# Copying both heads' transposed probabilities with ScalarE, and reordering the columns of the second block

## What is computed

```
h  = rms_norm(x,  norm_g[i]) * (1 + sc)  + sh        # tokens
hc = rms_norm(xc, norm_g[i]) * (1 + scc) + shc       # context
u, z  = split(h  @ w_in)                             # q, k, v and the gate z
uc, zc = split(hc @ w_in)
# per head: p = softmax(q k^T * scale (+ bias in kind B));  o = p v
# kind C: a = p0 - lambda * p1, o = a v, then rms_norm(o)
x  = x  + gt  * ((o  * silu(z))  @ w_out)
xc = xc + gtc * ((oc * silu(zc)) @ w_out)            # not in the last layer
```

## Time and profile before

| | |
|---|---|
| median of 3 runs | 2235.68 us (2224.66 to 2236.77) |
| the profiled execution's own time | 2232.29 us |
| its span in the trace | 2230.5 us |
| mean granted TensorE clock | 0.951 of full speed |
| busy: PE, DVE, ACT, POOL | 2036.7, 1187.7, 1084.9, 933.0 us |
| instructions: PE, DVE, ACT, POOL | 14528, 2582, 2073, 598 |

### The profile page before, as it was taken

One profiled execution on the slowest core, in us unless ns is written; L12 is line 12 of the kernel. 1 busy time (PEld: TensorE's weight loads), 2 busy tenths in 40 slices (PEclk: granted clock), 3 DMA queues, 4 the chain that ended last, 5 costly groups with the idle time before them and its releaser, 6 DMA issues.

```text
span 2230.5 us, 39126 instructions
## 1 busy us (share of the span) xinstructions
PE 2036.7 (91%) x14528; PEld 1717.4 (77%) x14528; DVE 1187.7 (53%) x2582; ACT 1084.9 (49%) x2073; POOL 933.0 (42%) x598
## 2 busy tenths in 40 slices
PE   6899899988998999888999999998999899798787
PEld 5898799987987899776766886665788667567666
DVE  6854556658545566347673206667223766614553
ACT  5353566453634654454554336445334555535443
POOL 1574378004744682043452123443204455424443
PEclk9899999998999999999999999999999999899898
DMA  7353656653435566442123332222223211223211
GB/s 262 114 152 112 190 172 196 184 186 113 149 101 187 171 188 188 164 142 76 48 61 101 114 104 84 88 67 85 95 86 95 95 38 48 76 95 104 67 58 57
DMA packets 72991, 262.89 MB, mean 118 GB/s; under 512 B 8048, under 2 KB 10224, under 8 KB 72560
## 3 DMA queue, kind: packets, MB, share of 16 engines
q1 hardware_dynamic: 71536, 256.31, 36.6%
q0 software_dynamic: 1280, 4.20, 0.6%
HBM read 259.43 MB, written 1.05 MB: 117 GB/s over the span
## 4 chain that ended last, share of the span: by engine, by line
PE 68%; DVE 9%; issue 8%; POOL 7%; ACT 6%; DMA 1%; DVEq 0%; SPq 0%; ACTq 0%; POOLq 0%
PE gemm L458 15%; PE gemm L459 14%; PE gemm L460 14%; PE gemm L740 7%; POOL w_lo L298 3%; PE tbank L696 2%; PE score L781 2%; PE obank L839 2%; PE stat L703 1%; POOL rot L1970 1%; PE gemm L666 1%; PE stat L536 1%; ACT w_hi L1018 1%; PE stat L754 1%; PE score L786 1%
## 5 line engine op out<-in xcount | busy, mean ns | idle before, releaser
L298 POOL TENSOR_TENSOR w_lo<-ring,w_hi 128x1024 fp32r<-128x1024 f32 x262 | 628.6, 2401 | 721.8 <-ACT w_hi L1018 718.4
L458 PE MATMUL gemm<-g_hi,w_hi 128*128 128x256 f32 x1344 | 394.7, 294 | 29.2 <-DVE w_lo L298 10.8
L1018 ACT ACTIVATE w_hi<-ring 128x1024 fp32r<-128x1024 f32 x344 | 361.3, 1053 | 82.9 <-PE gemm L460 37.4
L458 PE MATMUL gemm<-h_hi,w_hi 128*128 128x512 f32 (+1 forms) x928 | 390.8, 421 | 4.7 <-POOL w_lo L298 4.7
L459 PE MATMUL gemm<-g_lo,w_hi 128*128 128x256 f32 x1344 | 384.0, 286 | 0.0
L460 PE MATMUL gemm<-g_hi,w_lo 128*128 128x256 f32 x1344 | 383.6, 285 | 0.0
L459 PE MATMUL gemm<-h_lo,w_hi 128*128 128x512 f32 (+1 forms) x928 | 352.6, 380 | 0.0
L460 PE MATMUL gemm<-h_hi,w_lo 128*128 128x512 f32 (+1 forms) x928 | 352.1, 379 | 0.0
L458 PEld LDWEIGHTS gemm<-g_hi,w_hi 128*128 128x128 f32 x1344 | 262.9, 196 | 47.7 <-issue 23.3
L460 PEld LDWEIGHTS gemm<-g_hi,w_lo 128*128 128x128 f32 x1344 | 264.2, 197 | 0.0
L459 PEld LDWEIGHTS gemm<-g_lo,w_hi 128*128 128x128 f32 x1344 | 263.3, 196 | 0.1
(11 more groups left out here) (305 smaller groups left out, 3608.9 us busy)
## 6 DMA issues: line engine op xcount, KB each, us to landing
ring<-wall SPq DMA_DIRECT2D x478, 512.0 KB, 3.7
r<-nbias POOLq DMA_DIRECT2D x16, 256.0 KB, 2.9
cst<-consts SPq DMA_DIRECT2D x1, 2037.0 KB, 13.4
r<-x_t SPq DMA_DIRECT2D x1, 1024.0 KB, 5.8
x<-ctx_t SPq DMA_DIRECT2D x1, 1024.0 KB, 15.8
y_t<-x SPq DMA_DIRECT2D x4, 256.0 KB, 2.4
cst<-consts SPq DMA_DIRECT2D x1, 303.5 KB, 3.0
x<-pos SPq DMA_DIRECT2D x1, 128.0 KB, 2.0
```

The costliest lines, as they stand in the source:

```text
L298: eng.tensor_tensor(w_lo[:, q % SPLITS, :, :], ring[:, t % RING, :, :], w_hi[:, q % SPLITS, :, :].bitcast(F), ALU.subtract)\
L458: pe.matmul(out, w[0][:, k, :], x[0], start=start, stop=False)
L1018: act.activation(w_hi[:, q % SPLITS, :, :], ring[:, t % RING, :, :], ACT.Copy).then_inc(S["hi_ready"], 1)
```

## The change

Only `block2` is touched.

- `first_keys` and `second_keys` become one function, `pair_keys`, on ScalarE. The copy of an even unit stands ahead of the two exponentials of the next pair, that of an odd unit behind them.
- TensorE transposes an even unit ahead of the scores of the next pair, and no longer between two pieces of the chunks.
- ScalarE does `evac_q(c + 1)` at the beginning of unit NU // 2, and no longer at its end. With NU = 6 that is u = 3, ahead of `pair_keys(c, 1)` (kind C: ahead of `keys` and `subln`). With NU = 4 it is u = 2, ahead of `pair_keys(c, 0)` and the exponentials.
- In column 0 of the first three layers the eight steps of the `q` chunk are all done in the first four of twelve pieces (kind C: the first two of six).
- In the last column VectorE does `split_gated` for two units at a time.
- At a layer's beginning the context half of every odd m is scaled and shifted by ScalarE, and ScalarE waits for all of `h_ctx` before the first `h_hi`.

```diff
@@ TensorE
-                        if 0 < c < KC - 1 or not slot:
+                        if c == 0 and slot and spot < parts // 2:
+                            steps = KC * 3 // parts * (spot < parts // 3)
+                        elif 0 < c < KC - 1 or not slot:
...
                     for u in range(NU):
+                        past = [(c, u)] + past[:3]
                         if u % 2 == 0:
+                            if kind != "C" and past[2]:
+                                to_keys(*past[2])
                             scores(c, u)
                         gemm_part()
-                        past = [(c, u)] + past[:3]
-                        if past[2] and closes(kind, us[past[2][1]]):
+                        if past[2] and u % 2:
                             to_keys(*past[2])
@@ ScalarE
+                    if m % 2:
+                        act.activation(h2[:, m, T:N2], h2[:, m, T:N2], ACT.Identity, bias=ada[:, L, m, 1:2], scale=mod[:, m, 1:2])\
+                            .then_inc(S["h_ctx"], 1)
...
                 act.wait_ge(S["h_full"], (6 + L) * KC)
+                act.wait_ge(S["h_ctx"], (L + 1) * KC)
                 for m in range(KC):
-                    act.wait_ge(S["h_ctx"], L * KC + m + 1)
...
-                def second_keys(c, u):
+                def pair_keys(c, u):
 
                     pair = (c * NU + u) // 2
                     act.wait_ge(S["t_ready"], tbase(L) + c * NU + u + 1)
                     act.wait_ge(S["o_ready"], obase(L) + pair)
-                    act.activation(pt[:, 1, :], tb[:, :], ACT.Copy).then_inc(S["t_read"], 1)
+                    act.activation(pt[:, u % 2, :], tb[:, :], ACT.Copy).then_inc(S["t_read"], 1)
...
+                        if u == NU // 2 and c + 1 < KC:
+                            evac_q(c + 1, early if c == 1 else None)
+                            if c == 1 and slot:
+                                ada_columns_out()
+                        past = [(c, u)] + past[:3]
                         if u % 2 == 0:
+                            if kind != "C" and past[2]:
+                                pair_keys(*past[2])
                             exponential(c, u)
                             exponential(c, u + 1)
-                        past = [(c, u)] + past[:3]
                         if kind != "C":
                             if past[2] and u % 2:
-                                second_keys(*past[2])
+                                pair_keys(*past[2])
...
-                        if u == NU // 2 and c + 1 < KC:
-                            evac_q(c + 1, early if c == 1 else None)
-                            if c == 1 and slot:
-                                ada_columns_out()
@@ VectorE
-                            if past[2] and u % 2 == 0:
-                                first_keys(*past[2])
...
-                        if c == KC - 1:
-                            for i in splits_at(NU, u, FILL_SLOT[L], OT):
-                                split_gated(i)
+                        if c == KC - 1 and u % 2:
+                            for v in (u - 1, u):
+                                for i in splits_at(NU, v, FILL_SLOT[L], OT):
+                                    split_gated(i)
@@ GpSimd
-                for m in range(KC):
+                for m in range(0, KC, 2):
                     pool.wait_ge(S["normed"], (5 + L) * KC + m + 1)
                     pool.tensor_scalar(h2[:, m, T:N2], h2[:, m, T:N2], mod[:, m, 1:2], ada[:, L, m, 1:2], ALU.mult, ALU.add).then_inc(S["h_ctx"], 1)
```

More of the change, by code:

```diff
@@ L1397, in block2 @@
                 else:
-                    second_keys(KC - 1, NU - 1)
+                    pair_keys(KC - 1, NU - 2)
+                    pair_keys(KC - 1, NU - 1)
                 gated_high(KC - 1)
@@ L1804, in normalise @@
                     ins.then_inc(S["p_normed"], 1)
[L1806 to L1811, removed]
                 def output(c, u):
@@ L1898, in block2 @@
                     output(*last[-1])
-                else:
-                    first_keys(*last[-2])
                 gate_out(KC - 1)
```

## The result

| | before | after |
|---|---|---|
| median of 20 runs each | 2230.69 us (2221.81 to 2241.65) | 2239.35 us (2228.57 to 2246.35) |
| ratio, 95% interval | | 1.0038 [1.0025, 1.0050] |
| the profiled execution's own time | 2232.29 us | 2244.3 us |
| its span | 2230.5 us | 2242.2 us |
| mean granted TensorE clock | 0.951 | 0.951 |

What follows compares the result with a forecast made beforehand. PE was taken to bound L = 0 and nearly L = 1, while L = 2 and 3 wait for `evac_q`. Terms 14.5 + 25.8 - 22.4 + 0.5 - 11.5 + 1.5 - 1 = +7.4 us gave 2239.7 to 2243.1, forecast 2241, range 2230 to 2250.

Steps and rivals of the forecast that it cites:

- the same, on its upper side: Whole kernel: 2241 us, sum +7.4 us, within the 0.5% (11 us) a measurement can't tell from no change; chance 0.45.
- L = 0, columns 0, 1, 2 to 6: L = 0: early `evac_q` and tiling switches cost +1.5 and +1.2 us, then 2.25 a column, +11.3.
- L = 1, columns 0, 1, 2 to 6: L = 1: column 0 +1.5 us, column 1 +2.5, columns 2 to 6 4.3 each, +21.5, clock falls included.
- L = 2, columns; end: L = 2: earlier `evac_q` saves 1.7 us in six columns, -10.2; two splits go behind `combine` at the end, -1.3.
- L = 3, columns: L = 3: earlier `evac_q` removes the `q_sums` wait, saving 3.2 us (2.2 to 4.1) in each of seven columns, -22.4.
- beginnings: Layer starts: ScalarE's context activations delay its last token half by 0 to 0.5 us; four layers +1.5 (0 to +2).
- ends of L = 0, 1, 3 with the switches of column 7: Column 7: +0.6 us (L = 0), +0.3 (L = 1), +0.5 (L = 3's last column); ends of L = 0 and 1 -0.5 each.
- `evac_q` ahead of the odd copy: L = 0 and 1: `values_both` waits for the copy behind `evac_q`, stalling PE 1.6 us in L = 0, 3 in L = 1.
- The clock: L = 1: the clock falls behind the new stall in four of five columns, 1.7 us each, counted as 1.4 a column.
- The rival in which the clock falls in the columns 2 to 6 of L = 0 too: L = 0 adds 5 x 1.7 = +8.5 us, L = 3 saves only 15.4: +23, 2256 us; slower by over 0.5% given 0.40.
- The transposition ahead of the scores: Between `values_both` and scores: one more tiling change per pair, 0.2 us; 0.6 in a six-unit column, 0.4 in a four-unit one.
- the upper bound of 28.7: L = 3 saves the full 4.1 us in seven columns; part of the rival "faster", 2218 us, chance 0.15.

Runs made afterwards that it cites:

- Experiment 1: Changed kernel with `evac_q` late again, behind the odd unit's copy, in L = 0 and L = 1: 2209.61 us, ratio to the kernel before 0.9892.
- experiment 6: Kernel before with `evac_q` early, ahead of the odd unit's copy, in L = 0 and L = 1: 2254.2 us, ratio 1.0116.
- experiment 3: Kernel before with the even unit's transposition ahead of the scores, kinds A and B, copies left on VectorE and ScalarE: 2255.89 us, ratio 1.0118.
- 8: Changed kernel with `evac_q` late and transposition behind the scores in L = 0 and 1, old column 0 and beginnings: 2185.87 us, ratio to before 0.9799.
- Experiment 2: Kernel before with `evac_q` early in L = 3 alone, VectorE keeping its copy: 2212.0 us, ratio 0.9909.
- Experiment 7: Kernel before with `evac_q` early in L = 2 and L = 3 alone: 2197.5 us, ratio 0.9830.
- experiment 5: Kernel before with both copies on ScalarE, kinds A and B, transpositions and `evac_q` where they were: 2238.24 us, ratio 1.0010.
- experiment 4: Kernel before with only the beginnings changed, ScalarE scaling and shifting the context half of every odd m: 2236.75 us in one run.
- 9: The version of 8 with the changed beginnings added: 2188.98 us, ratio to the kernel before 0.9799.
- 10: The version of 8 with the changed order of column 0 added: 2184.48 us, ratio to the kernel before 0.9795.

## Why the prediction was right, and where its terms were off

The forecast was 2241 us, "the same, on its upper side"; measured were 2239.35 on a median of before of 2230.69, which is +8.7 where the sum said +7.4. The two spans differ by 11.7. The sum's terms, against the traces:

| term | forecast | trace |
|---|---|---|
| L = 0, columns 0, 1, 2 to 6 | +1.5, +1.2, +11.3 | +4.1, 0.0, +10.3 |
| L = 1, columns 0, 1, 2 to 6 | +1.5, +2.5, +21.5 | +3.6, +3.1, +18.9 |
| L = 2, columns; end | -10.2; -1.3 | -5.6; -3.1 |
| L = 3, columns | -22.4 | -26.6 |
| beginnings | +1.5 | +3.7 |
| ends of L = 0, 1, 3 with the switches of column 7 | +0.4 | +3.4 |

The signs of the large terms are right: L = 0 and 1 lose by the place of `evac_q`, L = 2 and 3 gain by it. That the total came within 4 us is partly luck. The terms that were too low (both columns 0, column 1 of L = 1, the columns of L = 2, beginnings, ends) miss 15 us together, and those that were too high 11, so they nearly cancel. (Two small slips of the sums change nothing: the parts of a column of L = 3 add up to 13.2 and not 13.1, and the high end of the range comes to 2260 by its own terms and not 2258.)

**`evac_q` ahead of the odd copy** was the dear step, as said. The forecast had the copy done 5.8 us behind the scores in L = 0 and a stall of 1.6; the timeline has 5.8 and 1.64. Experiment 1 takes it away alone and experiment 6 makes it alone. In L = 1 the stall is the 3 us that were forecast (3.1).

**The clock.** Its fall was counted for four of five columns of L = 1 and for none of L = 0, and that is what the trace shows: columns 2 to 5 of L = 1, and a mean of 1.00 in L = 0. The rival in which the clock falls in the columns 2 to 6 of L = 0 too didn't come. The working had no reason for four of five; that this came true is luck. The price was put too high: a column with the fall takes 27.1 us and one without 26.16, so a fall is worth 0.95 us and not 1.7. Without it a column is 3.0 longer, where 2.9 was said; this is why the columns 2 to 6 came out at +18.9 and not +21.5. The Trainium skill (TensorE: Matmul & The Clock Gate, HAM oscillation) describes waits of about 3 to 5 us that come round in every tile and throttle every one. Here waits of 3.1 us did so in four of five columns, and waits of 1.64 in none. But the waits of 1.6 us in L = 2 before the change had a lower clock behind them in all of columns 2 to 6, as in the earlier trace rows, so the length of a wait alone doesn't say it.

**The transposition ahead of the scores** was put at 0.2 us a pair; experiment 3 gives 0.22 in L = 0, where nothing else changes. With both copies on ScalarE (experiment 1 against 8) it is 0.15. The trace agrees with what the Trainium skill says of a drain at a change of tiling (TensorEngine Tiling (Array Packing), Key Properties).

**L = 3** saved 26.6 us, near the upper bound of 28.7 and not at the middle; over columns 2 to 6 it is 4.3 a column on average, where 4.1 was thought the most. A column of PE comes to 12.73 us where the sum of its parts said 13.1, and PE, busy 63.00 of 63.00 us, is its bound now. Experiment 2 shows that VectorE's copy was not the cause of the gain.

**L = 2** is the term that was mis-sized. The fall of the clock went with the wait, as said: the mean is 1.00 over columns 2 to 6. The limit fits what was named, VectorE's rotation behind `gate_out`, then the maximum. The waits of PE in its columns after are the two that the working asks for, for the rotated queries and for the exponentials, once a column each:

```profile
PE score L781 <- DVE d L1503: 4.9, 6, 0.8
PE score L781 <- ACT pr L1349: 4.8, 6, 0.8
```

A column fell from 24.05 to 22.72, 1.33 and not 1.7. And I multiplied by six columns, though column 1, whose evacuation has no weight part, was at 22.59 already and gave nothing, and column 2 gave 0.77; column 0 got 0.5 longer. The rest of that layer, its end, gained 3.1 in place of 1.3, and that isn't noise: it takes 98.0 to 99.7 us in the seven traces with the old order of `split_gated` and 95.5 to 95.8 in the five with the new one. Experiment 7, which has the early `evac_q` and the old splits, is at 98.1, so the splits are worth some 2.5 us, twice what was given.

**Column 0** of L = 0 and 1 was sized too low (1.5 against 4.1 and 3.6). The step missed the clock. PE waits 3.48 us (L = 0) and 5.17 us (L = 1) at `values_both` there, and what follows runs at the lower level:

```profile
1018.86 1.98 PE L839 MATMUL obank<-pt,arena 128*64 128x128 f32 x16 [3.48 <-ACT pt L1312]
...
1404.14 1.98 PE L839 MATMUL obank<-pt,arena 128*64 128x128 f32 x16 [5.17 <-ACT pt L1312]
```

That is 1.98 us for what takes 1.09 in the columns behind. Before, column 0 of L = 1 had the full clock throughout. With `evac_q` late again (experiment 1) the two columns are 2.25 and 2.05 us shorter. Where the eight steps are spread (experiment 6) the early `evac_q` costs column 0 of L = 0 only 1.0. It fits that filling the earlier wait with all eight steps left none for this one, but no run has the early `evac_q` with that one step undone. Column 1 of L = 0, on the other hand, cost nothing where 1.2 was counted; experiment 5 shows the copies on ScalarE alone saving 1.3 us there, which the working did not count.

**The beginnings** cost more than the 0 to 0.5 us a layer that were given: 0.2 to 1.6, +3.7 in all, and 3.5 and 3.6 in experiments 4 and 9. The order of the pieces explains 0.8 us a layer at its last token half. The clock adds to it. In the beginning of L = 3 it is low for 10.2 us in the changed kernel and in experiments 1 and 9 (1.6 to 2.0 us longer), and for 6.8 in the nine other traces; in that of L = 1 it is low for 10.2 us in experiment 4 alone (1.5 longer), and for 6.8 in the eleven others. Two windows that start 0.8 us behind the first normed activation of L = 3, before and after:

```profile
2016.00:2028.00 12.00, 11.25 (x64) 10.43 (x64) 9.02 (x15) 10.93 (x21) 5.10 (x9) 0.72 0.28 104
...
2052.00:2064.00 12.00, 10.34 (x51) 9.75 (x52) 8.07 (x14) 11.67 (x25) 2.23 (x4) 0.57 0.28 109
```

**Column 7 and the ends** cost 3.4 us where 0.4 was given, 2.7 of it in L = 1. From its last factor on, L = 1 takes 94.6 or 94.7 us in the changed kernel and experiment 1, and 90.3 or 90.4 in experiments 5, 8, 9 and 10, which also have both copies on ScalarE but transpose behind the scores. So the transposition ahead of the scores costs 4.3 us there, and the term had 0.3 for it.

## What to carry to other kernels

When an instruction is moved ahead on an in-order engine, list what it now stands in front of, and ask who waits for that: the same call that takes away a wait of 2.6 us a column in the layer with four units costs 1.6 to 4 in kinds A and B with six, because there it lands ahead of the copy that the bound engine waits for. A total near zero can be two large effects; one number per column and layer, read from an instruction that comes once in each, shows them at once and says which half to keep. Here keeping it was worth 2%. Middle columns mostly repeat to 0.1 us from trace to trace and are safe to read so; beginnings and ends of the same code differ by up to 2 us, and want several traces.

## What the runs showed of the hardware that was not expected

The same waits of PE did not always have the same price. In experiment 6 columns of L = 1 with the same order took 25.0 or 26.57 us, by whether the clock fell behind the wait of 1.8 us; in the changed kernel, behind waits of 3.1, the fall was worth 0.95.

VectorE's scaling of a probability block (L1813) takes 0.49 us by itself, and 2.58 us where it starts just behind GpSimd's `w_lo`, from the after kernel's timeline:

```profile
1112.68 2.35 POOL L298 TENSOR_TENSOR w_lo<-ring,w_hi 128x1024 fp32r<-128x1024 f32 x1 [5.75 <-ACT w_hi L1022]
1112.73 2.58 DVE L1813 TENSOR_SCALAR pr<-pr,small 128x512 f32<-128x512 f32 x1
```

It starts 0.05 us behind GpSimd's and ends 0.28 behind it, as if it had waited. What counted here was the order of the two starts. In this trace six executions that started inside a `w_lo`, with no other work of GpSimd beside them, took 0.75 to 2.62 us, and each ended 0.28 or 0.29 us behind it. Nine that started 0.24 to 0.30 us ahead of one took their 0.49 and ran beside it. The one shown was off PE's path.
